# Expert blocks: rows gathered in quarters and transposed on VectorE, empty slots skipped in the gather and in the scatter of results, guest weights copied by ScalarE

## What is computed

```python
def hierarchical_moe(h, w_rg, b_rg, w_re, b_re, w_gate, w_up, w_down):
    ...
    expert_ids = grp[:, None] * EXPERTS_PER_GROUP + top_idx
    ...
    def block_ffn(args):
        xb, e = args
        return (jax.nn.silu(xb @ w_gate[e]) * (xb @ w_up[e])) @ w_down[e]
    ys = lax.map(block_ffn, (rows, block_expert)).reshape(P, D) * row_w[:, None]
    out = jnp.zeros((n_tok + 1, D), ys.dtype).at[row_tok].add(ys)[:n_tok]
    return out.reshape(Bsz, T, D)
```

## Time and profile before

| | us |
|---|---|
| median of 3 runs | 3232.83 (3229.73 to 3238.44) |
| the profiled execution | 3227.49 |
| its span on the core | 3225.9 |
| granted TensorE clock, mean | 0.982 of full speed |

### The profile page before, as it was taken

How to read it: one execution, slowest core, us unless ns; L and a number is a source line. 1 busy time by engine, 2 the same in 40 slices (tenths; PEclk the granted TensorE clock), 3 DMA queues, 4 the chain that set the end, 5 groups by cost and what they waited for, 6 DMA issues and landing times.

```text
span 3225.9 us, 30362 instructions
## 1 busy us (share of the span) xinstructions
PE 3055.8 (95%) x12214; PEld 1629.6 (51%) x12214; DVE 1601.0 (50%) x2659; ACT 938.6 (29%) x1766; POOL 245.8 (8%) x174
## 2 busy tenths in 40 slices
PE   7999999899999999999999998899999998699997
PEld 3456557566664444444444454675846643333332
DVE  6467677466653555544564422312366525443334
ACT  4112462477772100000000001212335613222223
POOL 1000231000000000000000000000000000234431
PEclk9999999999999999999999999999999999799999
DMA  6113213000003211111121020000120013599994
GB/s 244 52 65 131 79 53 118 1 1 1 1 27 132 93 49 39 51 41 40 43 90 36 27 94 27 20 30 20 50 69 1 27 52 119 185 358 358 360 336 177
DMA packets 61512, 298.19 MB, mean 92 GB/s; under 512 B 14826, under 2 KB 21242, under 8 KB 39868
## 3 DMA queue, kind: packets, MB, share of 16 engines
q1 hardware_dynamic: 45244, 271.05, 23.2%
q0 software_dynamic: 16128, 25.21, 2.2%
HBM read 365.32 MB, written 31.55 MB: 123 GB/s over the span
## 4 chain that ended last, share of the span: by engine, by line
PE 85%; ACT 7%; DVE 6%; issue 1%; DMA 1%; another core or an unknown queue 0%; POOL 0%; SPq 0%; DVEq 0%; ACTq 0%; POOLq 0%
PE ps L1385 16%; PE ps L1512 8%; PE ps L2943 7%; PE ps L1687 6%; PE ps L906 5%; PE ps L2965 3%; PE ps L1309 3%; PE ps L2448 3%; PE ps L1689 3%; PE ps L1059 3%; PE ps L763 3%; PE ps L909 2%; PE ps L1087 2%; PE ps L2206 2%; ACT arena L1138 2%; PE ps L1071 1%
## 5 line engine op out<-in xcount | busy, mean ns | idle before, releaser
L1385 PE MATMUL ps<-arena 128*128 128x512 f32 x1232 | 529.6, 592 | 1.0 <-DVE arena L1416 1.0
L1385 PEld LDWEIGHTS ps<-arena 128*128 128x128 f32 x1232 | 233.3, 189 | 297.3 <-issue 287.4
L1512 PE MATMUL ps<-arena 128*128 128x512 f32 x616 | 264.5, 592 | 0.0
L2943 PE MATMUL ps<-arena 128*64 128x512 f32 x1024 | 229.6, 600 | 5.2 <-DMA arena<-in_wgu_dram,arena 5.2
L1687 PE MATMUL ps<-arena 128*128 128x512 f32 x480 | 209.5, 597 | 0.0
L1193 DVE TENSOR_SCALAR_CACHE_REDUCE arena<-ps 128x1280 f32<-128x1280 f32 x96 | 139.3, 1489 | 111.9 <-PE ps L1059 111.9
L1512 PEld LDWEIGHTS ps<-arena 128*128 128x128 f32 x616 | 116.6, 189 | 147.8 <-issue 143.7
L906 PE MATMUL ps<-arena 128*128 128x512 f32 (+1 forms) x432 | 173.6, 555 | 0.7 <-DVE arena L389 0.7
L2109 POOL COPY arena<-arena 64x512 f32<-64x512 f32 x8 | 5.6, 695 | 1887.1 <-DVE arena L2102 1886.8
L1687 PEld LDWEIGHTS ps<-arena 128*128 128x128 f32 x480 | 91.0, 191 | 114.1 <-issue 114.1
L2943 PEld LDWEIGHTS ps<-arena 128*64 128x64 f32 x1024 | 73.8, 137 | 138.2 <-issue 138.2
(11 more groups left out here) (432 smaller groups left out, 4553.8 us busy)
## 6 DMA issues: line engine op xcount, KB each, us to landing
arena<-in_wgu_dram SPq DMA_DIRECT2D x32, 2048.0 KB, 8.4
arena<-in_wed_dram SPq DMA_DIRECT2D x32, 1024.0 KB
arena<-in_wmod_dram SPq DMA_DIRECT2D x24, 1024.0 KB, 4.9
arena<-in_wup_dram SPq DMA_DIRECT2D x22, 1024.0 KB, 4.8
arena<-in_wout_dram SPq DMA_DIRECT2D x16, 1024.0 KB, 4.9
yslot<-arena SPq DMA_DIRECT2D x32, 512.0 KB, 9.6
arena<-in_wdn_dram SPq DMA_DIRECT2D x16, 704.0 KB, 4.1
arena<-in_w2b_dram SPq DMA_DIRECT2D x9, 1024.0 KB, 4.9
```

The source lines that it names most:

```text
L1385: ins = mm(bk(b), left[:, k], right[:, k], k == 0, k == 3)
L1512: ins = mm(bk(b), sb(left + k * 128, 128), right(k), k == 0, k == 10)
L2943: ins = mm(bk(b, 512, *rows), sb(XB + i % 2 * 1024 + k * 128 + 64 * side, 64), sb(w + k * 512, 512), k == 0, k == 7)
```

## The change

Rows and results:

- Each block's rows are fetched by four gathers instead of one. `x_q` views `xtok` as 4096 rows of 256 values. Quarter a of block i serves slots 32a to 32a+31: partition 32b+s gets piece b of the token in slot 32a+s. So VectorE can transpose 32x32 pieces (one `transpose` instruction of 128x1024 from XG to XB), and `pe_ex` and the two copies from PSUM go. The rows of the gate and up weights are laid out to match, on the host.
- The indices are made from `slots`: four 128x128 matmul calls spread each quarter's slots over the partitions, VectorE adds the piece number, and rounds to integers. An empty slot gets an index above 4095 and is skipped (`bounds_check`).
- Results go to `yslot` by an indirect DMA that GpSimd issues (`pool_outcome`), with an index of 65536 more for an empty slot, which is skipped. SP no longer writes results. Since part of `yslot` is then never written by the blocks, SP fills all 16 MB of it with constants, in four DMAs at the start of `sp_ffn` (`sp_slot_rows`).
- ScalarE makes the copy of 128x4096 for the guest (`act_guest_gu`), first thing in its iteration; VectorE's `dve_guest_gu` goes.

```diff
+    def sp_slot_rows():
+        for q in range(4):
+            LD.ready()
+            dma.dma_start(out=ys_d[q * 1024:(q + 1) * 1024].rearrange("(n p) f -> p n f", p=128),
+                          in_=sb(M_C, 1024).rearrange("p (u f) -> p u f", u=1).broadcast_to([128, 8, 1024])).then_inc(*LD.turn(("ysfill", q)))
...
     def sp_ffn():
+        sp_slot_rows()
         S.wait_ge(*(yield ("val", NU - 1)))
...
+        P.wait_ge(*(yield ("slots",)))
+        for a in range(4):
+            ins = mm(bk(b, NBLK, off=NBLK * a), every[:, 128 * a:128 * a + 128], slots, True, True)
...
     def dve_place():
+        vt.tensor_scalar(quarter, con("pidx"), 1 / 32, -31 / 64, MUL, ADD).then_inc(*V.step())
+        vt.tensor_copy(every.rearrange("p (a b s) -> p a b s", a=4, b=4),
+                       ident.rearrange("p (a u s) -> p a u s", a=4, u=1).broadcast_to([128, 4, 4, 32])).then_inc(*V.step(("every",)))
+        dve_round(quarter)
+        vt.tensor_scalar(quarter, quarter, 8192.0, None, ADD).then_inc(*V.step())
         V.wait_ge(*(yield ("cumrank",)))
...
+        V.wait_ge(*(yield ("spread",)))
+        vt.tensor_scalar(sidx, bk(bank["spread"], 4 * NBLK), quarter, None, ADD).then_inc(*V.step())
+        vdone()
+        vt.tensor_copy(sidx.bitcast(U32), sidx).then_inc(*V.step(("sidx",)))
...
-    def pool_rows(i):
+    def pool_rows(i, quarters):
         if i > 1:
-            G.wait_ge(*(yield ("ex", i - 2, 1)))
+            G.wait_ge(*(yield ("xb", i - 2)))
+        for a in quarters:
+            GD.ready()
+            gt.indirect_dma_start(sb(XG + i % 2 * 1024 + a * 256, 256), None, x_q, by_row(sidx.bitcast(U32)[:, NBLK * a + i:NBLK * a + i + 1]),
+                                  bounds_check=4095, oob_is_err=False).then_inc(*GD.turn(("xg", i, a)))
+
+    def pool_outcome(i):
...
+        for h2 in range(2):
+            G.wait_ge(*(yield ("eyc", i, h2)))
         GD.ready()
-        gt.indirect_dma_start(sb(XG + i % 2 * 1024, 1024), None, x_d, by_row(slots.bitcast(U32)[:, i:i + 1])).then_inc(*GD.turn(("xg", i)))
+        gt.indirect_dma_start(ys_d, by_row(be.bitcast(U32)[:, i:i + 1]), sb(YB + i % 2 * 1024, 1024), None,
+                              bounds_check=NSLOT - 1, oob_is_err=False).then_inc(*GD.turn(("ys", i)))
...
-        yield from pool_rows(0)
-        yield from pool_rows(1)
         G.wait_ge(*(yield ("widx",)))
+        G.wait_ge(*(yield ("sidx",)))
+        yield from pool_rows(0, (0, 1, 2, 3))
+        yield from pool_guest_gu(0)
+        yield from pool_rows(1, (0, 1, 2, 3))
         for i in range(NBLK + 1):
             if i + 2 < NBLK:
-                yield from pool_rows(i + 2)
-            if i < NBLK:
+                yield from pool_rows(i + 2, (0, 1))
+            if 0 < i < NBLK:
                 yield from pool_guest_gu(i)
+            if i + 2 < NBLK:
+                yield from pool_rows(i + 2, (2, 3))
             if i:
                 yield from pool_guest_dn(i - 1)
+            if i > 1:
+                yield from pool_outcome(i - 2)
+        yield from pool_outcome(NBLK - 1)
...
     def act_experts():
         for i in range(NBLK + 2):
             if i < NBLK:
-                if i > 1:
-                    A.wait_ge(*(yield ("egu", i - 2)))
-                A.wait_ge(*(yield ("ex", i, 1)))
-                st.activation(sb(XB + i % 2 * 1024 + 512, 512), bk(1), ACT.Copy).then_inc(*A.step(("xb", i, 1)))
+                yield from act_guest_gu(i)
...
-                V.wait_ge(*(yield ("ex", i, 0)))
-                vt.tensor_copy(sb(XB + i % 2 * 1024, 512), bk(0)).then_inc(*V.step(("xb", i, 0)))
+                for a in range(4):
+                    V.wait_ge(*(yield ("xg", i, a)))
+                vt.transpose(sb(XB + i % 2 * 1024, 1024).rearrange("p (k a s) -> p a k s", k=8, a=4),
+                             sb(XG + i % 2 * 1024, 1024).rearrange("p (a k s) -> p a k s", k=8, a=4)).then_inc(*V.step(("xb", i)))
...
-            if i < NBLK:
-                yield from dve_guest_gu(i)
...
-            if i >= 2:
-                S.wait_ge(*(yield ("eyc", i - 2, 0)))
-                S.wait_ge(*(yield ("eyc", i - 2, 1)))
-                LD.ready()
-                dma.dma_start(out=ys_d[(i - 2) * 128:(i - 1) * 128, :], in_=sb(YB + i % 2 * 1024, 1024)).then_inc(*LD.turn(("ys", i - 2)))
```

More of the change, by code:

```diff
@@ L2584, in build @@
     didx16 = room(16)
+    sidx, quarter, every = room(4 * NBLK), room(1), room(512)
     FS = marks["end"]
@@ L2686, in pe_route @@
         held[b] = [("widx",)]
+        b = next(banks)
+        yield from claim(b)
+        P.wait_ge(*(yield ("slots",)))
+        for a in range(4):
+            ins = mm(bk(b, NBLK, off=NBLK * a), every[:, 128 * a:128 * a + 128], slots, True, True)
+        bank["spread"] = b
+        ins.then_inc(*P.step(("spread",)))
+        held[b] = [("sidx",)]
     def act_gates(tc):
@@ L2905, in pool_rows @@
+    def pool_outcome(i):
+        for q in range(4):
+            G.wait_ge(*(yield ("ysfill", q)))
+        G.wait_ge(*(yield ("yidx",)))
+        for h2 in range(2):
+            G.wait_ge(*(yield ("eyc", i, h2)))
         GD.ready()
-        gt.indirect_dma_start(sb(XG + i % 2 * 1024, 1024), None, x_d, by_row(slots.bitcast(U32)[:, i:i + 1])).then_inc(*GD.turn(("xg", i)))
+        gt.indirect_dma_start(ys_d, by_row(be.bitcast(U32)[:, i:i + 1]), sb(YB + i % 2 * 1024, 1024), None,
+                              bounds_check=NSLOT - 1, oob_is_err=False).then_inc(*GD.turn(("ys", i)))
@@ L2920, in pool_experts @@
                 yield from pool_guest_gu(i)
+            if i + 2 < NBLK:
+                yield from pool_rows(i + 2, (2, 3))
             if i:
                 yield from pool_guest_dn(i - 1)
-    def pe_ex(i):
-        for h2 in range(2):
-            yield from claim(h2)
-            P.wait_ge(*(yield ("xg", i)))
-            for k in range(4):
-                ins = turn(bk(h2, 128, off=k * 128), sb(XG + i % 2 * 1024 + (4 * h2 + k) * 128, 128), ident)
-            ins.then_inc(*P.step(("ex", i, h2)))
-            held[h2] = [("xb", i, h2)]
+            if i > 1:
+                yield from pool_outcome(i - 2)
@@ L2971, in pe_experts @@
         for i in range(NBLK + 2):
-            if i < NBLK:
-                yield from pe_ex(i)
             if i >= 2:
@@ L3103, in pool_final @@
     def pool_final():
-        for i in range(NBLK - 15, NBLK):
+        for i in range(NBLK):
             G.wait_ge(*(yield ("ys", i)))
```

27 lines of the change are left out of this document (16 added, 11 removed).

## The result

The changed kernel takes 3245.00 us in the median, the kernel before 3232.83 beside it; the ratio is 1.0035 (95%: 1.0021 to 1.0048), slower by a third of a per cent. The forecast was 3209.5 us: **wrong, and wrong in sign**. The profiled execution of after has a span of 3243.4 us, 17.5 more than before.

What follows compares the result with a forecast made beforehand. TensorE was taken to bound the blocks at 11.70 us each, DMA near its edge. Terms: -25.2 (shorter periods) + 1.4 (start) + 0.5 (end) = -23.3 us, so 3232.8 became 3209.5 us; range 3202 to 3228.

Steps and rivals of the forecast that it cites:

- A: Rival: GpSimd's seven DMAs per block become the bound, slower; 3302 us at 2.0 us each, 3510 at 3.03; chance 0.07.
- The fill: At the start, SP's 16.8 MB of constants into yslot: 42 us long at 400 GB/s, over before the next weights, cost zero.
- D: Rival: the constants written at the start hold up TensorE's instruction fetches, 0 to 40 us; at 20, 3230 us; chance 0.07.
- The 25.2 us: Expert blocks: TensorE's period falls by 0.87 us, from 11.70 to 10.83, in 29 groups.
- if nothing else becomes late: Expert blocks: condition on the 25.2 us gain, checked for GpSimd, ScalarE, the guest gate-up gather, DMA and VectorE.
- seven cost 9.0 us, 1.8 to spare: GpSimd per block: seven DMAs at 1.29 us each make 9.0 us, below the 10.83 us period.
- e+7 to e+8, 3 us early: Guest gate-up gather's landing, e being the end of a block's down matmuls; issued at e+4.5, due at e+11.2.
- The last sentence of the forecast: Wrong if a scatter costs GpSimd over 2.8 us, or the guest gather lands later than 6.7 us after issue.
- B: Rival: guest gather stays late in the blocks; landing of 7.1 us, period 11.23, gain only 13.6, 3221 us; chance 0.09.
- q0's silence in 2906.5 to 2910.0: Blocks' trace: only q1 moved data then, so an issue was taken to wait for what is queued ahead.
- 320 more per block: DMA in the blocks: packets of skipped rows at 9 ns each, 0.2 us per engine, no cost.
- The start: First gather issued at 2775.7, first gate matmuls at 2784.0, block 1 at 2799.5: +1.4 us (-1.0 to +3).

Runs made afterwards that it cites:

- the order by deadlines: Changed kernel with ScalarE's guest gate-up copy right behind silu, GpSimd's gathers issued by readers' deadlines, rows of block j+3 gathered in block j: 3214.14 us, ratio 0.9934.

## Why the prediction was wrong

**Right.** The period without the eight transposes is 10.84 (10.83 said), in after too wherever nothing is late. GpSimd's indirect DMAs cost 1.00 to 1.02 us at a pitch of 1.30, scatter and quarters included, so A is out. ScalarE's copy takes 3.61 us (3.66). VectorE's transpose takes 1.24. The fill costs nothing: it is issued at 559.7 us, where TensorE (L909) is 2.1 us later than in before, and at 612.6 us (L1085) it is 0.5 us later. So D is out. The end costs +0.8 (0.5).

**The step that failed first: a deadline left out.** The 25.2 us hung on the condition "if nothing else becomes late". I worked out when the guest *gate-up* gather must land and never asked the same of the guest *down* gather. Before it started 2.3 us ahead of SyncE's 2 MB load; the two more quarters and the scatter put it 2 us behind. It is the seventh DMA in GpSimd's row, and "seven cost 9.0 us, 1.8 to spare" said that GpSimd fits, not that its last one is in time. Its late landings cost some 12 us in the profiled execution.

**Then the landing.** "e+7 to e+8, 3 us early" assumed that what is queued ahead of the gather is all that counts. What comes behind it counts as well: beside the 2 MB load at e+7.4 a late one took 8.38 us in place of 6.7. Whether the two take turns packet by packet is not shown. And less time was left: the gather started at e+5.5, not e+4.5: GpSimd began the scatter some 1.5 us after e, not 0.65, 0.85 us after the copy of results ended, and everything behind moved with it, so that 5.7 us were left until e+11.2 and not 6.7. In the blocks of before no gate-up gather lands in less than 6.1.'s 6.7 us were the landing for a start 3.6 us ahead of the load; no row showed one for 2 us. The last sentence of the forecast named this condition. B had the mechanism, but only its mild form: a landing of 7.1 us each time, and neither the half clock, which nearly doubles the price, nor the down gather. So B ended at 3221 where the kernel came to 3245, and no rival on the other side was this one.

**The reading of the earlier trace rows.** I took q0's silence in 2906.5 to 2910.0 for a rule, that the queues do not take turns. The windows of 1 us show both moving in the same microsecond. What kept q0 silent there I did not test.

**The packets.** "320 more per block", and the 1008 of the expectations, took every skipped row for a packet. The pages of the profile give 624 in place of 432, 192 more in all. By their 9 ns each that is nothing; whether their number makes a gather late is open.

**The start.** First gather at 2779.4 instead of 2775.7, of which 2.7 us come from a stage ahead of the change; block 0 at 2788.0. Block 1 came at 2803.3 instead of 2799.5, and not for its gather: the end of block 0's gate matmuls, 2796.5 as modelled, reached SyncE and ScalarE at 2801.8, which is the open point above.

## What to carry to other kernels

When DMAs are added to a queue, write down for each one when it starts, what large load is issued around it, and when its reader needs it; the last in the row moves most. Issue a gather of tiny packets well ahead of the next big load: here 6.2 and 3.6 us ahead left no wait from 2875 us on, 2 us ahead left four gate-up gathers late and 2 us behind twelve down gathers, and even 3.6 and 4.3 us ahead failed now and then. Cutting the load's rows is no sure way: it helped in two kernels whose gathers were late (1.0035 to 0.9944, 1.0311 to 1.0192), did nothing to the time in two where they were not, and cost 0.5% in a fifth (1.0001 to 1.0047). And profile a kernel whose readers are in time by a microsecond more than once: one profile of before showed no late gather, and with twelve matmuls added that change nothing in the time there were two. An event that nobody on the critical engine needs may still stand, in another engine's list, ahead of one that it does need.

## What the hardware showed that I had not expected

- A stall of 3.0 us cost 3.0 more in half clock (10.07 for 7.11), and one of 2.2 us 1.7 (8.79 for 7.10). But in the kernel before with twelve more matmuls a stall of 3.0 us cost nothing more: the gate matmuls behind it took 7.11, at a clock share of 1.00.
- 144 packets of a wholly skipped gather took up to 14 us to land beside loads (25 packets of 16 KB, 0.41 MB, in one microsecond of it), and 2.1 alone.
- With the 2 MB load as four DMAs of 32 partitions in rows of 16 KB, 2825 to 3125 us moved 189 GB/s at a DMA share of 0.86. After, with the load as one DMA of 128 partitions, moved 309 at 0.87.
- The DMA share in the blocks was 0.99 before, where nobody waited, 0.85 after, where many did, and 0.89 in the order by deadlines, where from 2875 us on nobody did: no measure of being late.
